# Splitting the gate stage's products over two halves of TensorE's rows

## The reference

```python
h = h + out_product
e = rmsnorm(p[i] @ w_pe) * pe_g          # p[i]: 512 x 256
h = h + sigmoid(h @ w_pg) * e            # w_pg: 2048 x 2048, the gate stage
```

## Time and profile before

| | |
|---|---|
| time, median of 3 runs | 2655.87 us (2655.51 to 2656.34) |
| profiled execution | 2656.61 us |
| its span, first to last instruction | 2654.8 us |
| busy: PE, DVE, POOL, ACT | 99%, 56%, 42%, 36% |
| matmuls | 12104 |
| share of the chain of waits on PE | 93% |

### The profile page before, as it was taken

One profiled execution on the slowest core, in us unless ns is written; L12 is line 12 of the kernel. 1 busy time (PEld: TensorE's weight loads), 2 busy tenths in 40 slices (PEclk: granted clock), 3 DMA queues, 4 the chain that ended last, 5 costly groups with the idle time before them and its releaser, 6 DMA issues.

```text
span 2654.8 us, 34449 instructions
## 1 busy us (share of the span) xinstructions
PE 2621.5 (99%) x12104; PEld 2123.7 (80%) x12104; DVE 1492.2 (56%) x2388; ACT 964.4 (36%) x1524; POOL 1103.1 (42%) x456
## 2 busy tenths in 40 slices
PE   7999999999999999999999999999999999999999
PEld 5888877778888888888777788888888888888887
DVE  7788777550043267887775500443675787522743
ACT  5222244442153242222444421543421565422521
POOL 3444432234444444444322344444444454444442
PEclk9999999999999999999999999999999999999999
DMA  8222222233323332222222232333333232322222
GB/s 304 96 95 98 93 86 82 76 114 116 98 100 113 133 126 95 95 95 94 84 83 76 111 119 96 102 111 126 106 108 126 89 103 96 140 97 95 96 95 103
DMA packets 77667, 283.51 MB, mean 107 GB/s; under 512 B 8256, under 2 KB 14912, under 8 KB 73600
## 3 DMA queue, kind: packets, MB, share of 16 engines
q1 hardware_dynamic: 77568, 282.20, 31.4%
HBM read 265.36 MB, written 19.96 MB: 107 GB/s over the span
## 4 chain that ended last, share of the span: by engine, by line
PE 93%; DVE 4%; issue 2%; ACT 1%; POOL 0%; POOLq 0%; DVEq 0%; ACTq 0%
PE acc L1301 20%; PE acc L1303 20%; PE acc L1302 20%; PE sc L1301 4%; PE sc L1303 4%; PE sc L1302 4%; PE acc L1325 3%; PE acc L1327 3%; PE acc L1329 3%; PE sc L1325 3%; PE sc L1329 3%; PE sc L1327 3%; PE sc L1434 1%; PE att L1459 1%; PE tr L1448 1%
## 5 line engine op out<-in xcount | busy, mean ns | idle before, releaser
L404 POOL TENSOR_TENSOR WL<-raw,WH 128x1024 fp32r<-128x1024 f32 x452 | 1102.9, 2445 | 1527.9 <-ACT WH L416 1527.7
L1301 PE MATMUL acc<-XH,WH 128*128 128x512 f32 x2432 | 958.5, 394 | 4.7 <-DVE XL L763 3.5
L1303 PE MATMUL acc<-XH,WL 128*128 128x512 f32 x2432 | 948.7, 390 | 0.0
L1302 PE MATMUL acc<-XL,WH 128*128 128x512 f32 x2432 | 948.1, 390 | 0.0
L416 ACT ACTIVATE WH<-raw 128x1024 fp32r<-128x1024 f32 x452 | 474.0, 1056 | 1123.7 <-PE acc L1303 731.9
L1301 PEld LDWEIGHTS acc<-XH,WH 128*128 128x128 f32 x2432 | 457.8, 188 | 104.2 <-issue 5.6
L1303 PEld LDWEIGHTS acc<-XH,WL 128*128 128x128 f32 x2432 | 457.4, 188 | 96.6
L1302 PEld LDWEIGHTS acc<-XL,WH 128*128 128x128 f32 x2432 | 458.0, 188 | 94.1 <-issue 1.5
L763 DVE SCALAR_TENSOR_TENSOR Y<-tr,lv,Y 128x497 f32 (+7 forms) x240 | 176.6, 736 | 2.9 <-DVE T L842 2.9
L763 DVE SCALAR_TENSOR_TENSOR T<-tr,lv,T 128x498 f32<-128x498 f32 (+6 forms) x224 | 164.8, 736 | 0.0
L1301 PE MATMUL sc<-XH,WH 128*128 128x512 f32 x384 | 150.6, 392 | 0.0
(11 more groups left out here) (221 smaller groups left out, 2850.4 us busy)
## 6 DMA issues: line engine op xcount, KB each, us to landing
raw<-in_w SPq DMA_DIRECT2D x452, 512.0 KB, 3.5
h_spill<-H SPq DMA_DIRECT2D x12, 1024.0 KB, 6.2
H<-h_spill SPq DMA_DIRECT2D x12, 1024.0 KB, 7.3
a<-bias_band SPq DMA_DIRECT2D x16, 384.0 KB, 3.2
H<-in_x SPq DMA_DIRECT2D x4, 1024.0 KB, 9.4
bias_band<-bias_line SPq DMA_DIRECT2D x1, 3072.0 KB, 18.9
out<-H SPq DMA_DIRECT2D x3, 1024.0 KB, 8.2
a<-in_pin SPq DMA_DIRECT2D x3, 512.0 KB, 5.7
```

The costliest lines, as they stand in the source:

```text
L404: pool.tensor_tensor(WL[:, c], raw[:, c], WH[:, c].bitcast(F), ALU.subtract).then_inc(wl_ready, 1)
L1301: pe.matmul(bank, WH[:, c], xh, start=first, stop=False)
L1302: pe.matmul(bank, WH[:, c], xl, start=False, stop=False)
L1303: return pe.matmul(bank, WL[:, c], xh, start=False, stop=last)
```

## The change

Each gate matmul over 128 rows becomes two over 64: one over the array's upper rows (partitions 0 to 63), one over its lower rows. The two never work on the same output tile: while the upper half does tile p, the lower half does tile p - 1, and adds to the bank in which the upper half of tile p - 1 has been summed. For that, a slot's partitions 64 to 127 are loaded from the unit two before (`back=2`), and each load is two DMAs, in the whole kernel. The lower half runs one k-step behind the upper. During tile 0 the lower half does tile 15, in a bank of its own (`HELD`); the upper half of tile 15 is added there last. The other tiles rotate over three banks (`ROT`). A new semaphore, `top_done`, makes the lower half's first matmul in a bank wait for the upper half's last one there. The steps of ACT and DVE follow one tile later, the end of the stage is reordered, and `embed` uses other banks.

```diff
+        ROT, HELD = (G[0], G[1], SC[0]), SC[1]
+        EMBED = (SC[1], SC[0], TR[0], TR[1])
...
-            def load(v, s):
-                sp.dma_start(raw[:, s * UW:(s + 1) * UW],
-                             w[bass.ds(v, 1)].rearrange("a p n -> (a p) n")).then_inc(raw_in[s], 16)
+            def load(v, s, low=None):
+                c = slice(s * UW, (s + 1) * UW)
+                for h, unit in ((0, v), (1, v if low is None else low)):
+                    r = slice(h * HALF, (h + 1) * HALF)
+                    sp.dma_start(raw[r, c], w[bass.ds(unit, 1), r, :].rearrange("a p n -> (a p) n")).then_inc(raw_in[s], 16)
...
                 gate(0)
-                gate(1)
-                square(0)
-                for t in range(2, NT):
-                    prep(u0, PG0 + 2 * t)
+                for t in range(1, NT - 1):
+                    prep(u0, PG0 + 2 * t + 2)
                     square(t - 1)
-                    if t == NT - 1:
+                    if t < NT - 2:
+                        prep(u0, PG0 + 2 * t + 3)
+                    else:
 
                         for k in range(UT):
                             xhigh(k, tl(H, k), norm_col(ly + 1, k))
                     gate(t)
-                    if t < NT - 1:
-                        prep(u0, PG0 + 2 * t + 1)
                 act.wait_ge(w_used, u0 + LAYER_U)
                 prep(u0, PG0 + 2 * NT - 1)
-                for k in range(UT, UT + 3):
+                gate(NT - 1)
+                for k in range(UT, UT + 2):
                     xhigh(k, tl(H, k), norm_col(ly + 1, k))
+                square(NT - 2)
+                xhigh(UT + 2, tl(H, UT + 2), norm_col(ly + 1, UT + 2))
                 square(NT - 1)
...
                 def halve(t):
-                    taken(PG0 + 2 * t + 2)
-                    dve.tensor_scalar(tl(T, t % 2), QUAD[t % 4][:, :], 0.5, None, ALU.mult).then_inc(tile_out, 1)
+                    taken(PG0 + min(2 * t + 4, PG_U))
+                    dve.tensor_scalar(tl(T, t % 2), (ROT[t % 3] if t < NT - 1 else HELD)[:, :], 0.5, None, ALU.mult).then_inc(tile_out, 1)
...
+                sums(NT - 4)
+                for k in range(5):
+                    next_low(k)
+                sums(NT - 3)
+                halve(NT - 2)
+                halve(NT - 1)
+                scaled(NT - 2)
+                next_low(5)
+                gated(NT - 2)
+                scaled(NT - 1)
+                gated(NT - 1)
+                next_low(6)
+                next_low(7)
+                next_low(8)
+                next_low(9)
+                sums(NT - 2)
+                next_low(10)
+                sums(NT - 1)
+                for k in range(11, NT):
+                    next_low(k)
...
+            def row_mm(h, bank, s, kt, j, first, last):
+
+                r = slice(h * HALF, (h + 1) * HALF)
+                c = slice(s * UW + kt % UT * P, s * UW + (kt % UT + 1) * P)
+                wt, xt = ((WH, XH), (WH, XL), (WL, XH))[j]
+                return pe.matmul(bank[:, :], wt[r, c], xt[r, kt * S:(kt + 1) * S], start=first, stop=last)
+
+            def low_rest(s, half, bank):
+
+                for j in range(3):
+                    last = row_mm(1, bank, s, half * UT + UT - 1, j, False, j == 2)
+                last.then_inc(w_used, 1)
+
+            def rows_unit(u, s, half, top, low, before, done, x_first=None, held=False):
+
+                pe.wait_ge(wl_ready, u + 1)
+                opens, closes = (False, True) if held else (True, False)
+                for k in range(UT):
+                    kt = half * UT + k
+                    if x_first is not None:
+                        pe.wait_ge(xl_ready, x_first + (kt + 1))
+                    for j in range(3):
+                        top_mm = row_mm(0, top, s, kt, j, opens and kt == 0 and j == 0, closes and kt == NT - 1 and j == 2)
+                        if k:
+                            if kt == 1 and j == 0 and done is not None:
+                                pe.wait_ge(top_done, done)
+                            row_mm(1, low, s, kt - 1, j, done is None and kt == 1 and j == 0, False)
+                        elif before is not None:
+                            low_mm = row_mm(1, before[1], before[0], before[2] * UT + UT - 1, j, False,
+                                            before[2] == 1 and before[3] and j == 2)
+                    if k == 0 and before is not None:
+                        low_mm.then_inc(w_used, 1)
+                if half == 1:
+                    top_mm.then_inc(top_done, 1)
...
                 pe.wait_ge(tile_out, n0 + (N_PG + 2))
-                quad_tile(n0 + N_PG, u0 + PG0, 0, x0 + 2 * NT)
-                quad_tile(n0 + N_PG, u0 + PG0, 1)
+                pe.wait_ge(e_out, ly * NT + NT - 3)
+                rows_tile(u0 + PG0, 0, ROT[0], HELD, None, None, x0 + 2 * NT)
+                rows_tile(u0 + PG0 + 2, 1, ROT[1], ROT[0], HELD, ly * NT + 1)
                 pe.wait_ge(esum_ready, ly * NT + NT)
                 stat()
-                for j in (2, 3):
-                    pe.wait_ge(e_out, ly * NT + (NT - 4 + j - 1))
-                    quad_tile(n0 + N_PG, u0 + PG0, j)
-                quads(n0 + N_PG, u0 + PG0, 1)
+                pe.wait_ge(e_out, ly * NT + NT - 2)
+                rows_tile(u0 + PG0 + 4, 2, ROT[2], ROT[1], ROT[0], ly * NT + 2)
+                with pe.Fori(0, 2) as i:
+                    for q in range(6):
+                        pe.wait_ge(tile_out, n0 + (i * 6 + (N_PG + 3 + q)))
+                        rows_tile(u0 + (i * 12 + (PG0 + 6 + 2 * q)), 3 + q, ROT[q % 3], ROT[(q + 2) % 3], ROT[(q + 1) % 3],
+                                  i * 6 + (ly * NT + 3 + q))
+                pe.wait_ge(w_used, u0 + PG0 + 2)
+                rows_tile(u0 + PG0 + 30, 15, HELD, ROT[2], ROT[1], ly * NT + 15, None, True)
+                low_rest(3, 1, ROT[2])
```

More of the change, by code:

```diff
@@ L39 @@
 RING = 4
+HALF = P // 2
 A_U, KV_U, Z_U, OUT_U, PE_U, PG_U = 48, 8, 32, 32, 4, 32
@@ L197, in build @@
         w_used = sem("w_used")
+        top_done = sem("top_done")
         h_in = [sem(f"h_in{c}") for c in range(4)]
@@ L276, in _, with units @@
         def _(sp):
-            def load(v, s):
-                sp.dma_start(raw[:, s * UW:(s + 1) * UW],
-                             w[bass.ds(v, 1)].rearrange("a p n -> (a p) n")).then_inc(raw_in[s], 16)
-            def units(first, lo, hi, order=(0, 1, 2, 3)):
+            def load(v, s, low=None):
[3 more added lines that the diff above has]
+                    sp.dma_start(raw[r, c], w[bass.ds(unit, 1), r, :].rearrange("a p n -> (a p) n")).then_inc(raw_in[s], 16)
+            def units(first, lo, hi, order=(0, 1, 2, 3), back=0):
                 with sp.Fori(0, (hi - lo) // RING) as i:
@@ L285, in units, with first_units @@
                         sp.wait_ge(wl_ready, first + (i * RING + (lo + s + 1)))
-                        load(first + (i * RING + (lo + order[s] + RING)), s)
+                        v = first + (i * RING + (lo + order[s] + RING))
+                        load(v, s, first + (i * RING + (lo + order[s] + RING - back)))
+            def first_units(first, lo, count):
+                for s in range(RING):
+                    sp.wait_ge(wl_ready, first + lo + s + 1)
+                    v = first + lo + s + RING
+                    load(v, s, v - 2 if s >= 2 else v - 2 + count)
             def pair_units(first, lo, hi):
@@ L360, in _ @@
                 pair_units(u0, OUT0 + 8, PE0 - RING)
-                units(u0, PE0 - RING, PG0 + 12)
+                units(u0, PE0 - RING, PG0 - RING)
+                first_units(u0, PG0 - RING, PG_U)
+                units(u0, PG0, PG0 + 12, back=2)
                 for c in range(4):
@@ L365, in _ @@
                     if c < 2:
-                        units(u0, PG0 + 12 + 8 * c, PG0 + 20 + 8 * c)
+                        units(u0, PG0 + 12 + 8 * c, PG0 + 20 + 8 * c, back=2)
                     elif c == 2:
@@ L424, in prep_loop @@
             def prep_loop(first, lo, n, i, per):
-                act.wait_ge(raw_in[n % RING], first * (16 // RING) + (i * (16 * per // RING) + 16 * ((lo + n) // RING + 2)))
+                act.wait_ge(raw_in[n % RING], first * (32 // RING) + (i * (32 * per // RING) + 32 * ((lo + n) // RING + 2)))
                 act.wait_ge(w_used, first + (i * per + (lo + n + 1)))
@@ L1056, in _ @@
                 gated(0)
[L1057 to L1062, removed]
-                        sums(t - 2)
[L1064 to L1081, removed]
+                for t in range(1, NT - 2):
+                    halve(t)
+                    scaled(t)
+                    if t >= 2:
+                        sums(t - 2)
+                    gated(t)
+                sums(NT - 4)
[18 more added lines that the diff above has]
+                    next_low(k)
             xb = DEPTH * 3 * NT
@@ L1357, in quads, with rows_tile @@
                         quad_tile(n + i * 4, u + i * 8, j)
```

(9 more changed lines are left out.)

9 lines of the change are left out of this document (4 added, 5 removed).

## The result

The changed kernel took 2670.99 us (median of 4 runs, 2668.31 to 2672.31) against 2655.88 (4 runs, 2655.51 to 2656.34) for the kernel before: the ratio is 1.0055, 95% interval 1.0039 to 1.0071. It is slower, by 15.1 us in the medians, 0.55%.

A forecast was written before the change was run, and what follows sets the result against it. PE, busy 99% of the span, was taken to bound the kernel. Stream -16.4, lag +1.3, shape changes +1.5, stage end +3.3 and loads +0.5 gave -9.8 us from the median 2655.87: 2646.1 us, range 2641 to 2668.

The forecast's parts named there:

- stream term: Gate stages: 1536 pairs of 64-row matmuls at 216 ns instead of 226.7, a gain of 16.4 us (0 to 20.6).
- What bounds the kernel: Whole kernel: PE busy 99% of the span; only the time per matmul or new holes between matmuls can move it.
- The price of a pair: Gate stages: a pair of 64-row float32r matmuls costs 216 to 226.7 ns; 216 taken.
- The halves run side by side: PE: two row halves run fully side by side, weight loads too, judged from the attention scores' f32 pairs.
- the rival of 3010 us: Gate stages: halves don't run together at one column per cycle, 453 ns a pair, +348 us; chance 0.04.
- Lag and changes of shape: Gate stages: 3 more slots per layer, +1.3 us; 8 changes between 128-row and 64-row shapes, +1.5 us.
- The end of the stage: Gate stage's end: two tiles open, PE waits for XL 6 and `stat`; 2.0 us layer 0, 1.3 layer 1.
- Loads: Two DMAs per unit cost nothing except at the start, where SP issues more: +0.5 us (0 to 1.5).
- `top_done`, embed's banks, DVE one tile late: Gate stages: these new waits and moved steps cost nothing; an uncovered `top_done` wait would cost 3 us per 0.1 us.
- The range of its own: Whole kernel: the forecast's range, fixed terms 3 to 11 and stream -20 to -12, given as 2641 to 2654 us.
- the rate doesn't change: Gate stages: a pair still costs 226.7 ns, only the fixed 6.6 us are left, 2662.5 us; chance 0.30.

The follow-up runs named there:

- late_order: Kernel before, with ACT's and DVE's gate-stage steps in the changed kernel's order, one tile later, two tiles open at the end: 2660.80 us against 2656.94, ratio 1.0015.
- whole_loads: Changed kernel, with units outside the gate stages loaded by one DMA over 128 partitions again: 2662.62 us against 2656.94 for the kernel before, ratio 1.0021.
- split_and_late: Kernel before, with split loads and ACT's and DVE's late order, matmuls still over 128 rows: 2665.10 us against 2656.77, ratio 1.0028.
- changed_again: Changed kernel unedited, measured again on another chip than late_order and whole_loads: 2665.55 us against 2656.77 for the kernel before, ratio 1.0037.

## Why the prediction was wrong

It forecast 2646.1 us, 9.8 faster, and the kernel came out 15.1 slower, outside the range by 3 us. Without its stream term the forecast is 2662.5, still inside the range: of the 24.9 us between forecast and median, 16.4 are the stream, 4.8 the loads, 3.4 the part that no trace shows, and 0.3 the rest. Its steps:

1. *What bounds the kernel* was right: PE's stream sets the time in the gate stages, then and now, at the full clock.
2. *The price of a pair* is the step that failed: "Lower end: 213.3 + 3 = 216 ns, the nearest row of the same 64-row shape. I take 216 ns." Measured: 226.8 ns in the kernel, 227 by itself. The term of -16.4 us is 0. The row of the same shape was in another type, f32, in two passes of two cycles per column; the row of the same type was in another shape, and the type was what counted. The reasoning behind the choice, that the 13.4 ns are a limit on columns per ns, falls with the 256- and 384-column rows: a fixed 13.3 ns per instruction can't be a rate. Its row could not have spoken against a limit either: the two f32 streams together carried 2.3 columns per ns, no more than the 2.26 of one float32r stream, and a float32r pair needs twice that. "They are not a fixed gap between two instructions" rested on the half clock, where the pitch was 426.7 ns; that the gap doesn't show there doesn't mean that it isn't fixed at the full one. Nothing measured it at a second size at the full clock, and the trace of before has no float32r product with fewer columns.
3. *The halves run side by side*: right, with starts within 10 ns in the rows shown; the rival of 3010 us was out.
4. *Lag and changes of shape*: 1.3 + 1.5 = 2.8 predicted, 2.6 left over after late_order, as a difference between traces, so right as far as that goes. The seams show 0.31 to 0.33 us where 0.32 was said.
5. *The end of the stage*: 2.0 and 1.3 predicted, 2.01 and 1.70 measured in late_order. In the changed kernel `sums(15)` ended 12.7 us after the last gate matmul, as added up. Layer 1 was 0.4 too low.
6. *Loads*: "Nothing, except at the start", +0.5 us. In the profiled execution they cost 3.1 at the start and 2.2 in the output stages. The step counted SP's issues and the landing of one load in a quiet stretch; it didn't ask where the DMA engines are full, which is at the start and where H comes back, and what a load costs them. Its upper end of 1.5 us was too low.
7. *`top_done`, embed's banks, DVE one tile late*: nothing, as said; PE's list of waits has none for them in either gate stage.
8. *The range of its own* is added up wrongly: fixed terms of 3 to 11 and a stream of -20 to -12 give 2639 to 2655, not 2641 to 2654. Nothing hangs on it.

The rival that described what happened is "the rate doesn't change", 2662.5 us with a chance of 0.30. The whole_loads kernel, whose loads outside the gate stages are the old ones, loses 6.3 us in its gate stages, where the rival has 6.1 (6.6 without the start's 0.5). That its median of 2662.62 is so near 2662.5 is in part luck, since it was measured beside a kernel before of 2656.94: +5.7 us. What the rival lacked of 2670.99 are the loads and the 3.4 us that no trace shows. The rule that "TensorEngine Tiling (Array Packing)" of the Trainium skill gives under "Theoretical Speedup", gain only where a dimension is 64 or less, stood beside that rival, and this case's runs agree with it: at a depth of 128 two 64-row matmuls take the time of one.

Open stays why the start's loss comes in some executions and not in others (in the profiled ones of the first measurement and of split_and_late; by their times alone, in all four of the first measurement, in one of five in changed_again, in five of eight in split_and_late). No run was made for it. Nor is it shown what lengthens ACT's wait in layer 1's output stage beside the split loads, or why the gap of a float32r matmul is absent at the lower clock.

No version here beats the kernel before. At 256 and 512 columns of float32r the idea has nothing to give, since it gains only if a pair costs less than one whole matmul.

## What to carry to other kernels

Before splitting a matmul that fills the array, measure one pair of the exact type and shape. Here the halves ran side by side and the pair cost what one instruction costs, fixed part and all. Where a fixed cost per instruction is suspected, two column counts at the same clock tell it from a rate. A load in two half-height transfers isn't free though it moves the same bytes: look at the windows in which the DMA engines are already full.

## What the runs showed of the hardware

- A float32r matmul has a pitch of 13.3 ns beyond its columns with 256, 384 or 512 of them over 128 rows, and the same over 64 rows with 256 or 512; with 128 columns it is 112 ns in all. bf16 has 2.5 (215.8 ns for 512). In bf16, 4-byte steps of the moving operand bring 225.9 ns, those of the weights 215.8.
- Four 32-row matmuls of float32r run side by side in some 227 ns, as two of 64 rows do.
- With weights of 64 or 32 columns a float32r matmul of 512 takes some 232 ns, no less than with 128.
- float32r and bf16 matmuls in turn take 460 ns per two, 17.5 more than the two pitches.
- A unit loaded as two transfers of 64 partitions takes SP 0.47 us each to issue between 100 and 290 us (0.33 there for a whole one, before), and its 4 KB packets 254 ns in the median instead of 159. With the DMA engines full from 5 to 25 us, 294 to 328 GB/s were moved with split loads and 389 to 392 with whole ones.
